# First stage of a two-layer RWKV-7/Hyena MoE block: modulation columns kept on chip, token differences taken before scaling, decay mixing folded into its weights, first head's weights asked for early

## The reference, cut to what matters

```python
cond_x = jax.nn.silu(c)
cond_c = jax.nn.silu(c_ctx)[None]
mx = (cond_x @ ada_w[i] + ada_b[i])[:, None, :]
mc = (cond_c @ ada_w[i] + ada_b[i])[:, None, :]
sh1x, sc1x, g1x, sh2x, sc2x, g2x = jnp.split(mx, 6, -1)
...
hx = _rms_norm(x, norm_g[i, 0]) * (1.0 + sc1x) + sh1x
hc = _rms_norm(ctx, norm_g[i, 0]) * (1.0 + sc1c) + sh1c
...
xx = _centred_shift(h) - h          # 0.5 * (previous token + next token) - this token
xr, xw, xk, xv, xa, xg = (h + xx * mix[n] for n in range(6))
...
jnp.tanh(jnp.einsum('bld,zdr->zblr', xw, w1))       # decay, two directions, rank 64
jnp.einsum('bld,zdr->zblr', xa, a1)                 # in-context rate, two directions, rank 64
jax.nn.sigmoid(xg @ g1)                             # gate, rank 160
```

## Time and profile before

| | |
|---|---|
| median of three runs | 2083.32 us (2082.84 to 2089.72) |
| the profiled execution's own time | 2077.27 us |
| its span, first to last instruction | 2075.4 us |
| TensorE's mean granted clock over the span (share of full speed) | 0.942 |
| TensorE busy over the span | 1796.5 us, 87% |
| VectorE, ScalarE, GpSimd busy | 774.5, 536.4, 172.0 us |
| start of `rwkv_inputs` | 5.3 us |
| VectorE's last instruction in it | ends at 97.2 us |
| first matmul of `rwkv_heads` | 105.16 us |

### The profile page before, as it was taken

The page is one execution under the profiler, slowest core; times in us unless marked ns, Lnnn a source line. Parts: engine busy times, 40 slices in busy tenths (PEclk is TensorE's granted clock), DMA queues, the critical chain, the costliest instruction groups (busy, mean ns, idle before and its releaser), DMA issues. The chain is left out here.

```text
span 2075.4 us, 34418 instructions
## 1 busy us (share of the span) xinstructions
PE 1796.5 (87%) x13965; PEld 964.0 (46%) x13965; DVE 774.5 (37%) x1818; ACT 536.4 (26%) x985; POOL 172.0 (8%) x120
## 2 busy tenths in 40 slices
PE   2468977978978897999999997999887999999996
PEld 1235545545545545444444442658555444434442
DVE  0856676676676534411001101623654411101101
ACT  2125544544444412111111111231202111111111
POOL 0412012012011000000000000000420000000000
PEclk8779999989999996999999999999997999999999
DMA  7012232232333447999999997202443999999993
GB/s 257 25 37 86 91 93 84 93 97 85 93 94 107 149 139 302 420 428 428 429 429 429 428 411 276 74 25 82 178 165 136 421 429 428 429 429 427 429 420 134
DMA packets 105518, 504.06 MB, mean 243 GB/s; under 512 B 15976, under 2 KB 60760, under 8 KB 79600
## 3 DMA queue, kind: packets, MB, share of 16 engines
q1 hardware_dynamic: 105328, 502.23, 61.0%
q10 hardware_dynamic: 64, 0.06, 0.0%
HBM read 501.15 MB, written 1.11 MB: 242 GB/s over the span
## 5 line engine op out<-in xcount | busy, mean ns | idle before, releaser
L1959 DVE TENSOR_TENSOR arena<-banks,arena 128x512 f32<-128x512 f32 x32 | 22.1, 692 | 660.8 <-PE banks L1774 660.8
L1774 PE MATMUL banks<-arena 128*64 128x512 f32 x1024 | 226.3, 594 | 10.6 <-DMA arena<-in_moe_w_up 10.6
L1796 PE MATMUL banks<-arena 128*64 128x512 f32 x1024 | 226.8, 595 | 3.3 <-ACT arena L1890 3.3
L1765 PE MATMUL banks<-arena 128*64 128x512 f32 x1024 | 225.3, 592 | 3.3 <-DVE arena L1882 3.3
L754 PE MATMUL banks<-arena 128*128 128x512 f32 (+1 forms) x384 | 158.8, 551 | 0.7 <-ACT arena L1063 0.7
L1774 PEld LDWEIGHTS banks<-arena 128*64 128x64 f32 x1024 | 82.1, 137 | 153.0 <-issue 153.0
L1765 PEld LDWEIGHTS banks<-arena 128*64 128x64 f32 x1024 | 74.2, 137 | 147.8 <-issue 144.2
L1796 PEld LDWEIGHTS banks<-arena 128*64 128x64 f32 x1024 | 70.7, 137 | 154.4 <-issue 150.7
L1884 ACT ACTIVATE arena<-banks,arena 128x128 f32<-128x128 f32 x128 | 48.1, 455 | 339.8 <-PE banks L1754 339.8
L1754 PEld LDWEIGHTS banks<-arena 128*128 128x128 f32 x1024 | 120.7, 197 | 28.1 <-issue 24.3
L1754 PE MATMUL banks<-arena 128*128 128x128 f32 x1024 | 126.8, 284 | 3.5 <-DVE arena L1954 3.5
(11 more groups left out here) (376 smaller groups left out, 2561.3 us busy)
## 6 DMA issues: line engine op xcount, KB each, us to landing
arena<-in_moe_w_gate SPq DMA_DIRECT2D x64, 2048.0 KB, 14.9
arena<-in_moe_w_up SPq DMA_DIRECT2D x64, 2048.0 KB, 17.1
arena<-in_moe_w_down SPq DMA_DIRECT2D x64, 2048.0 KB, 13.4
arena<-in_ada_w SPq DMA_DIRECT2D x128, 192.0 KB, 2.8
arena<-in_ada_w SPq DMA_DIRECT2D x64, 256.0 KB, 3.5
arena<-in_rw_wrkv SPq DMA_DIRECT2D x24, 512.0 KB, 5.2
arena<-in_hy_w_in SPq DMA_DIRECT2D x6, 2048.0 KB, 8.3
arena<-in_ada_w SPq DMA_DIRECT2D x8, 1024.0 KB, 11.9
```

Of the source, the lines that this page charges most:

```text
L1765: mm = pe.matmul(G[j * CAP:(j + 1) * CAP, :], xT[:, t, j * CAP:(j + 1) * CAP], wg[par][j][:, t], start=(t == 0), stop=(t == KT - 1))
L1774: mm = pe.matmul(U[j * CAP:(j + 1) * CAP, :], xT[:, t, j * CAP:(j + 1) * CAP], wu[j][:, t], start=(t == 0), stop=(t == KT - 1))
L1796: mm = pe.matmul(bank[j * CAP:(j + 1) * CAP, :], hT[:, t, j * CAP:(j + 1) * CAP], wd[j][:, t, half * 512:(half + 1) * 512], start=(t == 0) ...
L1959: dve.tensor_tensor(h, U[:, :], sg, ALU.mult).then_inc(h_ready, 1)
```

## The change

The `constants` block is gone; its DMA is issued in `rwkv_inputs`, where TensorE waits for it. `ctx` and `x` are asked for first, each with a semaphore of its own, and the small vectors and the bias are asked for by ScalarE's queue. `FirstModulation` no longer writes its row to DRAM: ScalarE's queue copies it straight from the one partition into the columns `sc` and `sh` of 64 partitions, eight DMAs (`columns`). The first two of the modulation's eight pieces are multiplied before the transposes, six after them; tile 0 goes through bank 1. The transposed tokens are copied out of PSUM unscaled, by ScalarE and VectorE in turn; VectorE takes the differences `xx` of the unscaled tokens, with `add_bias` between its two instructions, and scale and shift are put on afterwards, tile by tile: the tokens by VectorE, the differences by ScalarE, and the two edge columns of each tile, where the missing neighbour has no shift, get half the shift taken off by a small VectorE instruction. The decay's mixing is dropped: GpSimd multiplies `w1` by its mixing coefficients (`w1m`), and TensorE computes `w1` times the tokens plus `w1m` times the differences, 16 matmuls where there were 8. The loads of the first head pair are issued at the end of the first stage's SyncE stream, into places that `RwkvTensors` now reserves.

```diff
     def load_weights(self, sp):
         ada = self.ins["ada_w"].rearrange("l (p t) n -> l p t n", t=KT)
-        for q in range(self.PARTS):
-            sp.dma_start(self.bias[q * 32:(q + 1) * 32, :],
-                         self.ins["ada_b"][0, q * 512:(q + 1) * 512].partition_broadcast(32)).then_inc(self.bias_in, 16)
         for t in range(KT):
             sp.dma_start(self.w[t], ada[0, :, t, 0:FIRST]).then_inc(self.ada_in[t], 16)
...
-    def store(self, act):
+    def columns(self, act):
         act.wait_ge(self.row_ready, 1)
         for q in range(self.PARTS):
+            dst = (self.shift, self.scale)[q // 2]
             for i in range(2):
-                act.dma_start(self.mods[0, i, q * 512:(q + 1) * 512].unsqueeze(0),
-                              self.row[q * 32 + i:q * 32 + i + 1, :]).then_inc(self.row_out, 16)
+                act.dma_start(dst[q % 2 * 64:q % 2 * 64 + 64, 1 - i, :],
+                              self.row[q * 32 + i:q * 32 + i + 1, :].rearrange("o (p t) -> o p t", t=KT)).then_inc(self.cols_in, 16)
...
         @block.sync
         def _(sp):
+            sp.dma_start(ctxn, ins["ctx"].rearrange("b (i p) d -> p (b i) d", p=P)).then_inc(ctx_in, 16)
+            sp.dma_start(s.x_res, ins["x"].rearrange("b (i p) d -> p (b i) d", p=P)).then_inc(x_in, 16)
             first.load_conditions(sp)
+            sp.dma_start(s.const[:, :], ins["const"]).then_inc(const_in, 16)
+            first.load_weights(sp)
...
+            r.load_first(sp, ins, 0)
+            r.load_values(sp, ins, 0)
...
         @block.scalar
         def _(act):
+                act.dma_start(rows[n * CH:(n + 1) * CH, :], v.rearrange("(m p) -> m p", p=P)).then_inc(rows_in, 16)
+            act.dma_start(mix, ins["rw_mix"][0].rearrange("n (p t) -> p n t", t=KT)).then_inc(vec_in, 16)
+            act.dma_start(ng, ins["norm_g"][0, 0].rearrange("(p t) -> p t", t=KT)).then_inc(vec_in, 16)
+            first.load_bias(act)
             first.sigmoid(act)
...
-            first.store(act)
+            for k, t in enumerate(turn_order):
+                if k % 2 == 0:
+                    act.wait_ge(turned, k + 1)
+                    act.activation(inner(t), both(turned_bank(t)[:, :]), ACT.Copy).then_inc(raw_act, 1)
+            first.columns(act)
+            act.wait_ge(diff_ready, 1)
             act.wait_ge(scale_ready, 1)
-            for k, t in enumerate(turn_order):
-                act.wait_ge(xnT_done, k + 1)
+            for t in range(KT):
                 for i in range(2):
-                    act.activation(hT[:, t * 2 + i, 1:L + 1], s.psum[t][:, i * L:(i + 1) * L], ACT.Identity,
-                                   bias=sh[:, i, t:t + 1], scale=sc[:, i, t:t + 1]).then_inc(hT_ready, 1)
+                    act.activation(xx[:, t * 2 + i], xx[:, t * 2 + i], ACT.Identity, scale=sc[:, i, t:t + 1]).then_inc(diff_scaled, 1)
...
         @block.tensor
+            first.products(pe, s.psum[0], range(2, KT))
+            pe.wait_ge(w_in, 32)
+            pe.wait_ge(folded, 1)
             for t in range(KT):
+                pe.wait_ge(tile_ready, t + 1)
+                pe.matmul(both(s.psum[2][:, :]), w1[:, t].rearrange("p a b -> p (a b)"), inner(t), start=(t == 0), stop=False)
+                mm = pe.matmul(s.psum[2][:, :], w1m[:, t], xx[:, t * 2:t * 2 + 2].rearrange("p a b -> p (a b)"), start=False, stop=(t == KT - 1))
...
         @block.vector
+            dve.wait_ge(raw_act, KT // 2)
+            dve.drain()
+            dve.tensor_tensor(xx, hT[:, :, 0:L], hT[:, :, 2:L + 2], ALU.add)
+            dve.drain()
             first.add_bias(dve, s.psum[0])
-            dve.wait_ge(vec_in, 6 * 16)
+            dve.scalar_tensor_tensor(xx, xx, 0.5, hT[:, :, 1:L + 1], ALU.mult, ALU.subtract)
+            dve.drain()
+            dve.sem_inc(diff_ready, 1)
+            dve.wait_ge(vec_in, 2 * 16)
+            first.wait_columns(dve)
...
+            for t in range(KT):
+                for i in range(2):
+                    v = hT[:, t * 2 + i, 1:L + 1]
+                    dve.tensor_scalar(v, v, sc[:, i, t:t + 1], sh[:, i, t:t + 1], ALU.mult, ALU.add)
+                dve.wait_ge(diff_scaled, 2 * t + 2)
+                v = ends[:, t * 2:t * 2 + 2, 0:L:L - 1]
+                dve.tensor_tensor(v, v, edge[:, t].unsqueeze(2).to_broadcast([P, 2, 2]), ALU.add)
+                dve.drain()
+                dve.sem_inc(tile_ready, 1)
+            for name in ("a", "g", "k", "r"):
                 mix_tokens(dve, name).then_inc(mixed, 1)
 
         @block.gpsimd
         def _(pool):
-            pool.wait_ge(xx_ready, 1)
+            pool.wait_ge(w_in, 32)
+            pool.wait_ge(vec_in, 2 * 16)
+            pool.tensor_tensor(w1m, w1.rearrange("p t a b -> p t (a b)"), mix[:, which["w"]].unsqueeze(2).to_broadcast([P, KT, 2 * RW_LORA]), ALU.mult)
+            pool.drain()
+            pool.sem_inc(folded, 1)
+            pool.wait_ge(tile_ready, KT)
```

More of the change, by code:

```diff
@@ L120, with __init__ @@
     PARTS = FIRST // 512
-    def __init__(self, s, ins, mods, low):
-        self.s, self.ins, self.mods = s, ins, mods
+    def __init__(self, s, ins, low, scale, shift):
+        self.s, self.ins, self.scale, self.shift = s, ins, scale, shift
         self.raw, self.sig, self.cond = s.take(2, KT), s.take(2, KT), s.take(KT, 32)
@@ L283, in rwkv_inputs @@
     xx = s.take(KT * 2, L)
[L284 removed]
+    xa, spare = s.take(KT, TOK), s.take(KT, TOK)
     xg = s.take(KT, L)
     w1, a1 = s.take(KT, 2, RW_LORA), s.take(KT, 2, RW_LORA)
+    w1m = s.take(KT, 2 * RW_LORA)
     g1 = s.take(KT, RW_GATE)
[L288 removed]
+    ctxn = spare.rearrange("p (i a) b -> p i (a b)", i=4)[:, 0:TT]
     xn = xa.rearrange("p (i a) b -> p i (a b)", i=4)[:, 0:TT]
@@ new lines, in _ @@
+            act.dma_start(mix, ins["rw_mix"][0].rearrange("n (p t) -> p n t", t=KT)).then_inc(vec_in, 16)
+            act.dma_start(ng, ins["norm_g"][0, 0].rearrange("(p t) -> p t", t=KT)).then_inc(vec_in, 16)
+            first.load_bias(act)
+            first.sigmoid(act)
+            for half, arrived in enumerate((ctx_in, x_in)):
+                act.wait_ge(arrived, 16)
+                for n in (2 * half, 2 * half + 1):
+                    src, i = tiles[n]
+                    act.activation(junk, src[:, i], ACT.Square, accum_out=stat[:, n:n + 1])
+                    act.drain()
+                act.sem_inc(sq_done, 1)
@@ new lines, in _ @@
+            for half in range(2):
+                act.wait_ge(var_done, half + 1)
+                v = stat[:, 2 * half:2 * half + 2]
+                act.activation(v, v, ACT.Sqrt).then_inc(root_done, 1)
+            for k, t in enumerate(turn_order):
[4 more added lines that the diff above has]
+            act.wait_ge(diff_ready, 1)
@@ L371, in _ @@
+            act.activation(r.gl[0:RW_GATE - P, 1], s.psum[4][0:RW_GATE - P, L:2 * L], ACT.Sigmoid)
         @block.tensor
         def _(pe):
+            pe.wait_ge(const_in, 16)
             pe.wait_ge(rows_in, 9 * 16)
             pe.transpose(s.psum[7][:, 0:9 * CH], rows[0:9 * CH, :], s.c("ident")[0:9 * CH, 0:9 * CH]).then_inc(chv_done, 1)
+            first.products(pe, s.psum[0], range(0, 2))
             pe.wait_ge(xn_ready, 4)
@@ L378, in _ @@
                 if t == 0:
-                    first.products(pe, s.psum[0])
-                    pe.wait_ge(first.row_ready, 1)
+                    pe.wait_ge(raw_act, 1)
                 for n in range(4):
                     src = xn[:, n, t::KT] if n < 2 else xx_n[:, n - 2, t::KT]
-                    mm = pe.transpose(s.psum[t][:, n * P:(n + 1) * P], src, s.c("ident"))
-                mm.then_inc(xnT_done, 1)
-            pe.wait_ge(w_in, 5 * 16)
-            pe.wait_ge(hT_ready, 2 * KT)
@@ new lines, in _ @@
+            mm.then_inc(lora_done, 1)
+            pe.wait_ge(a_in, 32)
+            pe.wait_ge(mixed, 1)
+            for t in range(KT):
+                mm = pe.matmul(s.psum[3][:, :], a1[:, t].rearrange("p a b -> p (a b)"), xa[:, t], start=(t == 0), stop=(t == KT - 1))
+            mm.then_inc(lora_done, 1)
+            pe.wait_ge(g_in, 16)
+            pe.wait_ge(mixed, 2)
+            for t in range(KT):
+                pe.matmul(s.psum[4][:, 0:L], g1[:, t, 0:P], xg[:, t], start=(t == 0), stop=(t == KT - 1))
@@ L397, in _ @@
+            for t in range(KT):
+                mm = pe.matmul(s.psum[4][0:RW_GATE - P, L:2 * L], g1[:, t, P:RW_GATE], xg[:, t], start=(t == 0), stop=(t == KT - 1))
             mm.then_inc(lora_done, 1)
@@ L523, in rwkv_heads @@
     s.at = r.heads
-    wkv = [s.take(KT, P) for _ in range(3)]
-    w2, a2 = s.take(P), s.take(P)
-    g2 = s.take(2, P)
+    wkv, w2, a2, g2, kr_in, v_in = r.wkv, r.w2, r.a2, r.g2, r.kr_in, r.v_in
     ka1 = s.take(CH)
```

187 lines of the change are left out of this document (86 added, 101 removed).

## The result

The changed kernel takes 2057.99 us, the median of four runs (2053.12 to 2059.92), against 2083.08 us (2077.44 to 2089.72) for the kernel before beside it: 0.9869 of it, with a 95% interval of 0.9842 to 0.9895. So the change gains 23 to 25 us, where 31 were forecast. The profiled execution took 2058.01 us. This is its span, and then its first stage, from the timeline (start, duration, engine, line, form, count, idle before and releaser); the lines answer to the earlier trace rows.

A forecast was written before the change was run, and what follows sets the result against it. The prediction took the first stage's single chain of four links, 105.16 us, as the price. Gains of 21.5 (stage), 7.5 (barrier) and 2.4 (clock) sum to 31.4 us, giving 2052 from the 2083.3 median; likeliest range 2046 to 2058 (0.70).

The forecast's parts named there:

- four signs by which the prediction would fall: Scale waiting for copies beyond 42, TensorE's g ending after VectorE's mixing, barrier waiting for SyncE, heads taking longer than before.
- The rival with the late columns: Column copies wait for bulk loads; scale ready at 47.5, 7.1 us later, total 2059; chance 0.18 with other small mishaps.
- Link 1, loads: First-stage loads: earlier ctx 5.4 us, constants 1.8 back, dip 1.2; last weight piece at 31.6 instead of 36.45.
- Link 2, row: Modulation: 1.9 us from the start of the last products to the bias's end; row ready at 33.5.
- Link 2, columns: Modulation row to columns: eight copies issued in 2.49 us, landing 3.1 us later at 39.1, hidden by the second difference.
- Link 2, the fold: GpSimd's w1 multiplication, 2.7 us, costs VectorE's second difference 1.8 us, ending it at 39.7; scale ready at 40.4.
- Link 3: Scaling by tiles shared by ScalarE and VectorE takes 7.8 us, bounds 6.6 and 9; mixing starts at 48.2, not 64.04.
- Link 4, mixing: VectorE's mixing without w's eight wide instructions takes 27.5 us against 33.13, paying 5.6; TensorE hidden by 2.4 us.
- Barrier: Between first stage and heads: 0.5 us remains of 8.0 as head loads are issued early; gain 7.5 us.
- Clock over the barrier: TensorE's gap before the heads shrinks to about 3.2 us, keeping full clock for the first products; gain 2.4 us.
- a bound TensorE: TensorE at half clock through the low-rank products ends the stage at 98.9; total 2077.5, no change; chance 0.03.
- a SyncE that sets the end: Eight small-piece loads at 13.29 us each hold SyncE; heads start at 114.4, total 2092.5, slower; chance 0.02.

The follow-up runs named there:

- old_loads: Changed kernel with the earlier load order: constants first and waited for, then all small loads on SyncE ahead of the modulation's pieces; 2063.65 us, ratio 0.9918.
- bulk_later: Changed kernel, but SyncE waits until the eight column copies have landed before asking for a1, g1 and the first head's weights; 2058.53 us, ratio 0.9874.
- head_loads_back: Changed kernel with the first head pair's loads back at the start of the heads' block; 2063.37 us, ratio 0.9885.
- start_wait_later: Changed kernel with TensorE's wait for VectorE's start-up of the heads moved behind the first head pair's first products; 2057.48 us, ratio 0.9865.
- w_mixed: Changed kernel with the decay's mixing back on VectorE, 8 TensorE matmuls instead of 16, no w1 fold on GpSimd; 2065.77 us, ratio 0.9904.
- best_warm: Changed kernel with columns by TensorE matmuls, the later wait for the heads' start-up, and three idle matmuls behind the gate's product; 2050.87 us, ratio 0.9858.
- pe_columns: Changed kernel with the eight column copies replaced by 16 small TensorE matmuls, VectorE reading scale and shift from PSUM; 2055.39 us, ratio 0.9868.
- after: First measurement of the changed kernel itself, against the kernel before; 2057.99 us, ratio 0.9869.
- after_again: Second measurement of the unaltered changed kernel, source of its second profile, against the kernel before; 2058.82 us, ratio 0.9881.

## Why the prediction was right, and where its sum was off

The direction held, most of the gain came where it was forecast, and the time came out 6 us above the number, at 2058 instead of 2052, on the edge of the likeliest range (2046 to 2058). The mechanism held only in part. Two of the four signs by which the prediction would fall occurred: the scale waited for the copies to 46.4, beyond 42, and behind the first head matmul the profiled execution took 1.8 us longer than before (the second is no more than what such profiles differ by). The rival with the late columns (2059) came closest, but it priced a wait for the bulk loads alone, and part of the lateness was the issue.

Part of the hit is luck. The sum was made for the profiled execution, 2045.9; that took 2058.01, some 12 us more: 8.0 of them ahead of the first head matmul, 4.2 behind it, where 2.4 us of the clock were to be gained. The forecast of 2052 added the 6 us by which the median of before lay above its profiled execution. In the changed kernel the median and the profiled execution agree (2057.99 and 2058.01), and this took half of the miss away.

Term by term, the sum put the first head matmul at 76.2; it came at 84.21, 8.0 us later.

- *Link 1, loads:* forecast 31.6 for the last piece, seen 32.96 at the products' start, just outside the bounds. `old_loads` prices the part at 3.0 to 3.9 us; 4.8 was too much.
- *Link 2, row:* forecast 33.5, seen 35.72, since the last products took 1.93 us and not 1.06: TensorE's clock had fallen in its wait for the pieces (mean 0.74 in 32 to 34 us). In the second profile they came at full clock, and the bias ended 0.9 us earlier. The sum took full clock for granted.
- *Link 2, columns: the term that was mis-sized.* The sum says "half of that, 3.1 us, is my value", and "2.49 us as for the writes". Issue took 5.08, and from its end to the use of the columns it was 4.9: 10.1 us from row to use, not 5.6. So what scale waited for was the copies, not the second difference. `bulk_later` shows that 2.6 us of the excess is the issue of the form; with the load away the landing alone took 1.9 us, less than the 3.1 of the sum, so the rest is the load beside it. Half of a write and a read of 6.1 us was no stand-in for a copy in 32-byte pieces issued into a full stream; that stream was also longer than before by the very loads that the change put behind it, which `head_loads_back` prices at 3.5 us.
- *Link 2, the fold:* 1.8 us forecast, 1.5 seen (5.94 against 4.42), but the steps behind it failed. The fold took 1.90 us, not 2.7, and VectorE isn't slowed by a factor of three here; it waits. Where GpSimd began first (35.41 against 35.64), the fold took its 1.90 us and the difference took 1.52 us more than its 4.42; where VectorE began first (34.55 against 35.12, `start_wait_later`), the difference took its 4.42 us and the fold 5.61. The Trainium skill ("SBUF — State Buffer", "Who interferes with whom") calls the port pair that the two share an exclusive lock, for which the order of issue decides who waits. These profiles agree: 1.5 us were lost by VectorE, most of the fold's remainder of 1.67, and the later fold ended 1.76 us behind the difference, nearly its whole 1.90. In the changed kernel it cost nothing, since the columns came later still.
- *Link 3:* 7.8 us forecast, 7.79 seen, but by another engine, so this hit is luck. The sum took ScalarE's 7.4 us and 0.4 for the last tile. ScalarE needed 6.49 and was done at 52.89; VectorE, put at 6.6 us and its tiny instructions, went on to 54.05, since a tile took it 0.95 us (53.24 to 54.19), 0.74 of them for the two scalings.
- *Link 4, mixing:* 27.5 forecast, 27.58 seen; w's part 5.6 and 5.5 (`w_mixed`). Two errors cancelled within it: GpSimd took 26.5 us, not 25.4 (its multiplications 15.36 instead of 14.41), and VectorE had 1.1 us left behind it, not 2.1. TensorE's chain ended at 78.4, 3.4 us before VectorE's; hidden, as forecast (2.4).
- *Barrier:* 0.5 forecast, 2.44 seen. The wrong step is "VectorE's own start-up in the heads is covered by TensorE's first products": TensorE's first product waits for that start-up (`ka_ready`). It had been covered by the loads that the change removed. `start_wait_later` shows 0.40 us without it.
- *Clock over the barrier, the term that failed:* forecast 2.4 us, seen 0.5 in the k product (9.07 against 9.58) and none in the first. The mean clock was 0.88 in 80 to 81 us, so it fell about 2.4 us behind TensorE's last matmul at 78.4, not 5; the gap itself was 5.8 us, not 3.2 (by the sum's own terms it would be 3.7, the 0.5 of the barrier being left out). One fall seen 5 us behind the last matmul was no ground for taking 3.2 us as safe. `best_warm` shows that the term exists and is larger: with 1.31 us of gap the two products take 1.13 and 7.13 us, 0.95 and 1.94 less than here. The 0.5 us for the first of them came from no row.

From 76.2 these make: scale 6.0 us late (46.40 instead of 40.4; the row 2.2, the columns behind it 3.9), barrier 1.9, the rest 0.1. Of the stage's 20.95 us, 19.3 show between the profiled executions, and 23 to 25 between the medians.

The rivals of a bound TensorE and of a SyncE that sets the end did not occur: SyncE issued its last load at 40, although it was held 19 us by a `w1` load.

## What to carry to other kernels

Whoever takes a wait away should look up what else the waiting engine waits for at that place: here an initialisation of 2 us was hidden by the very DMA wait that was removed. Loads asked for early share the DMA engines with the small transfer on the chain; either they wait for it, or the small transfer is done by an engine, as 16 matmuls of 2 us together replaced 10 us of copies. A part of a few microseconds is priced by a mark in the profile that lies right behind it, and not by the whole time.

## What the runs showed of the hardware

A DMA of 64 pieces of 32 bytes from one partition to 64 cost ScalarE's queue 0.62 us of issue, whether the DMA queues were full or empty; a write of the same 2 KB to DRAM had cost 0.3.

The scatter between executions of one kernel goes with TensorE's mean granted clock: `pe_columns` took 2051.90 us at 0.952 and 2066.67 us at 0.939. Over the 52 runs of the thirteen measurements, each set against the mean of its own four, the correlation is -0.81 and the slope 12.4 us for 0.01 of clock. The work is the same; the stretches at half clock fall in other places, as the rows of the granted clock on the pages of `after` and `after_again`, one and the same kernel, show. Gains of 2 to 5 us in the first stage are smaller than this scatter, and a single pair of kernels doesn't show them.

All the measurements together do. Over the thirteen of the table, a straight line of the median against the start of the first head matmul has a slope of 0.92 us for a microsecond (standard error 0.11, correlation 0.93), and 0.84 without the two kernels with idle matmuls. If the heads took longer the earlier they start, it would be near 0. So between 77 and 89 us what the stage gains comes through nearly whole, although the kernels ran on several chips and the line is no proof for any one of them.
